# Router logits in two halves, the first expert block gathered by channel halves, and one table for three further blocks

## The reference

```python
hn = rms_norm(x, norm_ffn[1])                      # (256, 1024)
logits = hn @ w_router                             # (256, 8)
top_logit, top_idx = lax.top_k(logits, 2)
gate = softmax(top_logit)
# tokens of each expert are laid into blocks; for each block, with its expert e:
y_blk = (silu(x_blk @ w1[e]) * (x_blk @ w3[e])) @ w2[e]     # w1, w3: 1024x2816, w2: 2816x1024
y[token] += gate * y_blk
x = x + y
```

## Time and profile before

| | us |
|---|---|
| median of 3 runs | 1583.64 |
| lowest and highest | 1582.43, 1583.94 |
| the profiled execution, its time | 1583.63 |
| the profiled execution, its span | 1581.8 |
| TensorE busy | 1483.3 (94%) |
| VectorE busy | 1241.0 (78%) |
| ScalarE busy | 895.2 (57%) |
| last projection matmul starts | 739.15 |
| first expert matmul starts | 766.16 |

### The profile page before, as it was taken

How to read it: one execution, slowest core, us unless ns; L and a number is a source line. 1 busy time by engine, 2 the same in 40 slices (tenths; PEclk the granted TensorE clock), 3 DMA queues, 4 the chain that set the end, 5 groups by cost and what they waited for, 6 DMA issues and landing times.

```text
span 1581.8 us, 21845 instructions
## 1 busy us (share of the span) xinstructions
PE 1483.3 (94%) x7397; PEld 1201.7 (76%) x7397; DVE 1241.0 (78%) x1325; ACT 895.2 (57%) x970; POOL 388.1 (25%) x490
## 2 busy tenths in 40 slices
PE   4989989999998999999899999999999999999996
PEld 3767768788877776677688888888888888888785
DVE  6888967655555789856688988889888898888986
ACT  5632344544455523244476776767767677776774
POOL 6979972910002299900000000000000000000000
PEclk9989999999998999998899999999999999999998
DMA  9421235565544412077399999999999999999980
GB/s 263 161 80 54 80 82 185 182 198 178 191 160 141 134 54 80 28 252 254 129 364 345 348 361 333 351 344 339 362 331 351 345 339 361 331 351 327 355 293 27
DMA packets 269146, 373.48 MB, mean 236 GB/s; under 512 B 12960, under 2 KB 216096, under 8 KB 268960
## 3 DMA queue, kind: packets, MB, share of 16 engines
q1 hardware_dynamic: 265520, 366.47, 68.5%
q0 software_dynamic: 1280, 3.16, 1.0%
q10 hardware_dynamic: 2288, 3.11, 0.6%
HBM read 371.65 MB, written 1.05 MB: 236 GB/s over the span
## 4 chain that ended last, share of the span: by engine, by line
PE 72%; DVE 16%; ACT 5%; issue 4%; POOL 1%; DMA 0%; DVEq 0%; ACTq 0%; POOLq 0%
PE bank L459 69%; DVE lo L1204 4%; ACT hi L864 3%; DVE raw L1303 2%; PE bank L477 1%; DVE raw L1284 1%; PE bank L794 1%; DVE raw L1283 1%; DVE bank L1294 1%; DVE raw L1293 1%; POOL raw L330 1%; DVE at_lo L1640 1%; DVE bank L1295 1%; DVE bank L1296 1%; DVE at_lo L1609 1%
## 5 line engine op out<-in xcount | busy, mean ns | idle before, releaser
L1204 DVE TENSOR_TENSOR lo<-raw,hi 128x2048 fp32r<-128x2048 f32 x347 | 804.5, 2323 | 168.9 <-ACT hi L864 159.6
L864 ACT ACTIVATE hi<-raw 128x2048 fp32r<-128x2048 f32 x347 | 662.9, 1914 | 92.3 <-PE bank L459 91.8
L459 PE MATMUL bank<-hi,at_hi 128*128 128x512 f32 x1280 | 521.2, 407 | 31.8 <-DVE at_lo L1609 7.8
L459 PE MATMUL bank<-hi,at_lo 128*128 128x512 f32 x1280 | 506.4, 396 | 0.0
L459 PE MATMUL bank<-lo,at_hi 128*128 128x512 f32 x1280 | 506.3, 396 | 0.0
L459 PEld LDWEIGHTS bank<-hi,at_hi 128*128 128x128 f32 x1280 | 245.1, 191 | 85.4 <-issue 18.0
L459 PEld LDWEIGHTS bank<-hi,at_lo 128*128 128x128 f32 x1280 | 244.6, 191 | 52.9
L459 PEld LDWEIGHTS bank<-lo,at_hi 128*128 128x128 f32 x1280 | 245.4, 192 | 46.8
L459 PE MATMUL bank<-hi,ht_hi 128*128 128x512 f32 x440 | 172.2, 391 | 4.5 <-DVE ht_lo L1541 3.5
L459 PE MATMUL bank<-lo,ht_hi 128*128 128x512 f32 x440 | 171.3, 389 | 0.0
L459 PE MATMUL bank<-hi,ht_lo 128*128 128x512 f32 x440 | 171.2, 389 | 0.0
(11 more groups left out here) (235 smaller groups left out, 1177.7 us busy)
## 6 DMA issues: line engine op xcount, KB each, us to landing
raw<-in_moe_w_dram SPq DMA_DIRECT2D x528, 512.0 KB, 5.6
raw<-in_ffn_w_dram SPq DMA_DIRECT2D x66, 512.0 KB, 4.3
raw<-in_w_in_dram SPq DMA_DIRECT2D x64, 512.0 KB, 4.7
raw<-in_w_branch_dram SPq DMA_DIRECT2D x16, 512.0 KB, 4.0
raw<-in_w_out_dram SPq DMA_DIRECT2D x16, 512.0 KB, 4.5
raw<-in_w_glu_dram SPq DMA_DIRECT2D x4, 512.0 KB, 4.0
xres<-in_x_dram SPq DMA_DIRECT2D x1, 1024.0 KB, 5.3
areg<-in_norm_mix_dram ACTq DMA_DIRECT2D x2, 512.0 KB, 5.6
```

The lines of the kernel that those rows point to most:

```text
L459: return pe.matmul(o, a, b, start=start, stop=stop)
L864: act.activation(hi[:, slot, :], src, ACT.Copy).then_inc(hi_ready, 1)
L1204: tt(lo[:, slot, :], src, hi[:, slot, :].bitcast(f32), SUB).then_inc(lo_ready, 1)
```

## The change

1. The logits go into bank 2 (`PY[0]`) and the slot numbers into bank 3 (`PY[1]`), with semaphores of their own (`logits_full`, `pos_full`), in place of two turns of the TR banks. `logits(0)` issues the 16 matmuls on channel blocks 0 to 3 before `norm_t(1, "h", 1)`, and `logits(1)` those on blocks 4 to 7 after the last `at_lo`.
2. `gather` raises `xe_full` after each bank. ScalarE and VectorE wait for, and report, each half by itself. TensorE waits for half 0 before `up(0, 0, 0)` and for half 1 before `up(0, 0, 1)`. In the loop it waits for both halves at the place of before, with counts twice as high.
3. The table: in place of three rounds of eight small instructions, all three further blocks are handled in each instruction, over 24 or 48 numbers in place of 8 or 16.

```diff
--- before.py
+++ after.py
@@ -63,7 +63,6 @@
                 names.append((l, "o", s - 1))
         names += [(l, "a", t) for t in range(2)] + [(l, "s", t) for t in range(2)] + [(l, "s2", t) for t in range(2)]
         names += [(l, "m", g) for g in GROUPS] + [(l, "h", g) for g in GROUPS]
-    names += ["router", "pos"]
     return {name: n for n, name in enumerate(names)}
 
 
@@ -201,6 +200,7 @@
         h_full, g_ready, h_done, ht_tr, ht_hi_ready, ht_lo_ready = (sem("h_full"), sem("g_ready"), sem("h_done"), sem("ht_tr"),
                                                                     sem("ht_hi_ready"), sem("ht_lo_ready"))
         ffn_done = sem("ffn_done")
+        logits_full = sem("logits_full")
         sel_ready, pos_full, routed, final_ready, stored = (sem("sel_ready"), sem("pos_full"), sem("routed"),
                                                             sem("final_ready"), sem("stored"))
         gate_exp, router_in, place_ready, pg_full, gt_ready = (sem("gate_exp"), sem("router_in"), sem("place_ready"),
@@ -312,9 +312,11 @@
         r_hot = piece(384, 32).rearrange("p (i t e) -> p i t e", i=2, t=2)
         sel = piece(416, 16).rearrange("p (t e) -> p t e", t=2)
         r_pos = piece(432, 16).rearrange("p (t e) -> p t e", t=2)
-        r_over, r_rank, r_one = piece(448, 8), piece(456, 8), piece(464, 8)
+        r_over, r_rank = piece(448, 8), piece(456, 8)
         r_tmp = piece(472, 16).rearrange("p (t e) -> p t e", t=2)
         r_tab = piece(488, 5)
+        x_one, x_name = (piece(c, 24).rearrange("p (k e) -> p k e", k=3) for c in (576, 600))
+        x_tmp = piece(624, 48).rearrange("p (t k e) -> p t k e", t=2, k=3)
         router = piece(512, 64).rearrange("p (k e) -> p k e", k=KD)
         router_parts = ht_hi[:, 0, 0:KD * 2 * NE].rearrange("p (k c) -> p k c", k=KD)
         place = vreg[:, 1, 0:256].rearrange("p (t s) -> p t s", t=2)
@@ -741,25 +743,30 @@
             mixer(1)
 
 
+            def logits(half):
+
+                for th in range(TH):
+                    for k in range(4 * half, 4 * half + 4):
+                        for i, a in enumerate((at_hi, at_lo)):
+                            m = mm(PY[0][:, th * 16:(th + 1) * 16], a[:, k, th * P:(th + 1) * P], router_parts[:, k, :],
+                                   k + th + i == 0, th + i == 2 and k == KD - 1)
+                return m
+
+            pe.wait_ge(at_lo_ready, at_count(1, "h", 2))
+            pe.wait_ge(router_ready, 1)
+            logits(0)
             norm_t(1, "h", 1)
             pe.wait_ge(at_lo_ready, at_count(1, "h", 3))
-            pe.wait_ge(router_ready, 1)
-            bank = open_turn("router")
-            for th in range(TH):
-                for k in range(KD):
-                    for i, a in enumerate((at_hi, at_lo)):
-                        m = mm(bank[:, th * 16:(th + 1) * 16], a[:, k, th * P:(th + 1) * P], router_parts[:, k, :],
-                               k == 0 and i == 0, k == KD - 1 and i == 1)
-            m.then_inc(tr_full, 1)
+            logits(1).then_inc(logits_full, 1)
             pe.wait_ge(sel_ready, 1)
-            bank = open_turn("pos")
+            bank = PY[1]
             pe.wait_ge(loads, 32)
             tri, ones = cst[:, C_TRI:C_TRI + P], cst[:, C_ONE:C_ONE + P]
             mm(bank[:, 0:8], tri, sel[:, 0, :], True, True)
             mm(bank[:, 8:16], tri, sel[:, 1, :], True, False)
             mm(bank[:, 8:16], ones, sel[:, 0, :], False, True)
             mm(bank[:, 16:24], ones, sel[:, 0, :], True, False)
-            mm(bank[:, 16:24], ones, sel[:, 1, :], False, True).then_inc(tr_full, 1)
+            mm(bank[:, 16:24], ones, sel[:, 1, :], False, True).then_inc(pos_full, 1)
 
 
             def gather():
@@ -768,7 +775,8 @@
                     for th in range(TH):
                         m = mm(banks[4 + k // 4][:, (k % 4) * P:(k % 4 + 1) * P], xn[:, th, k * P:(k + 1) * P],
                                place[:, th, :], th == 0, th == 1)
-                m.then_inc(xe_full, 1)
+                    if k % 4 == 3:
+                        m.then_inc(xe_full, 1)
 
             def up(b, c, half):
 
@@ -778,7 +786,7 @@
                 if half == 0 and c == NCH - 1:
                     pe.wait_ge(gt_ready, b + 1)
                 if half == 0 and c == NCH:
-                    pe.wait_ge(xe_lo_ready, b + 2)
+                    pe.wait_ge(xe_lo_ready, 2 * b + 4)
 
                 for k in range(4):
                     m = three(h_bank(c)[:, :], at_hi[:, 4 * half + k, 0:P], at_lo[:, 4 * half + k, 0:P],
@@ -840,8 +848,8 @@
 
             pe.wait_ge(place_ready, 1)
             gather()
-            pe.wait_ge(xe_lo_ready, 1)
             for half in range(2):
+                pe.wait_ge(xe_lo_ready, half + 1)
                 up(0, 0, half)
             expert_step(0, 0)
             last = pe.value_load(table[0:1, 0:1], min_val=NE - 1, max_val=MAXB - 1)
@@ -1142,10 +1150,10 @@
             act.activation(r_exp, r_diff, ACT.Exp).then_inc(gate_exp, 1)
 
             def gathered(n):
-                act.wait_ge(xe_full, n)
                 for g in range(2):
-                    m = act.activation(at_hi[:, 4 * g:4 * g + 4, 0:P], banks[4 + g][:, :].rearrange("p (k c) -> p k c", k=4), ACT.Copy)
-                m.then_inc(xe_hi_ready, 1)
+                    act.wait_ge(xe_full, 2 * n + (g - 1))
+                    act.activation(at_hi[:, 4 * g:4 * g + 4, 0:P], banks[4 + g][:, :].rearrange("p (k c) -> p k c", k=4),
+                                   ACT.Copy).then_inc(xe_hi_ready, 1)
 
             def silu(b, c):
                 act.wait_ge(tile_used, b * FFN_TILES + (T_MOE + (3 * c if c > 0 else 1) + 1))
@@ -1566,11 +1574,11 @@
 
             for th in range(TH):
                 ts(xn[:, th, :], xn[:, th, :], col(RI + th), None, MUL).then_inc(xn_scaled, 1)
-            bank = wait_turn(dve, "router")
+            dve.wait_ge(logits_full, 1)
+            bank = PY[0]
             sums = bank[:, 0:32].rearrange("p (t i e) -> p t i e", t=2, i=2)
             own.step(dve.tensor_copy(r_tmp, sums[:, :, 0, :]))
-            tt(r_logit, r_tmp, sums[:, :, 1, :], ADD).then_inc(tr_free[TURN["router"] % 2], 1)
-            wait_read(dve, "router")
+            own.step(tt(r_logit, r_tmp, sums[:, :, 1, :], ADD))
             for th in range(TH):
                 own.step(dve.max(r_best[:, th, :], r_logit[:, th, :]))
                 own.step(dve.max_index(r_index[:, th, :], r_best[:, th, :], r_logit[:, th, :]))
@@ -1590,13 +1598,14 @@
             for i, g in enumerate((r_g, r_exp)):
                 own.step(tt(r_hot[:, i, :, :], r_hot[:, i, :, :], g.unsqueeze(2).broadcast_to([P, 2, NE]), MUL))
             own.step(tt(cols[:, 1, :, 0:NE], r_hot[:, 0, :, :], r_hot[:, 1, :, :], ADD))
-            bank = wait_turn(dve, "pos")
+            dve.wait_ge(pos_full, 1)
+            bank = PY[1]
             pos = bank[:, 0:16].rearrange("p (t e) -> p t e", t=2)
             own.step(stt(r_pos, pos, 1.0, sel, ADD, MUL))
             own.step(ts(cols[:, 0, :, 0:NE], r_pos, -1.0, None, ADD))
 
-            ts(r_over, bank[:, 16:24], float(P), None, ALU.is_gt).then_inc(tr_free[TURN["pos"] % 2], 1)
-            wait_read(dve, "pos")
+            own.step(ts(r_over, bank[:, 16:24], float(P), None, ALU.is_gt))
+
             def places():
 
                 for th in range(TH):
@@ -1604,28 +1613,27 @@
                 return m
 
             def gathered(n):
-                dve.wait_ge(xe_hi_ready, n)
                 for g in range(2):
-                    m = tt(at_lo[:, 4 * g:4 * g + 4, 0:P], banks[4 + g][:, :].rearrange("p (k c) -> p k c", k=4),
-                           at_hi[:, 4 * g:4 * g + 4, 0:P].bitcast(f32), SUB)
-                m.then_inc(xe_lo_ready, 1)
+                    dve.wait_ge(xe_hi_ready, 2 * n + (g - 1))
+                    tt(at_lo[:, 4 * g:4 * g + 4, 0:P], banks[4 + g][:, :].rearrange("p (k c) -> p k c", k=4),
+                       at_hi[:, 4 * g:4 * g + 4, 0:P].bitcast(f32), SUB).then_inc(xe_lo_ready, 1)
 
             own.step(dve.tensor_copy(column, cols[:, :, :, 0]))
             places().then_inc(place_ready, 1)
             own.step(dve.tensor_tensor_scan(r_rank, cst[:, C_ONE:C_ONE + NE], r_over, 0.0, MUL, ADD))
+            own.step(tt(x_one, r_rank.unsqueeze(1).broadcast_to([P, 3, NE]),
+                        cst[:, C_IOTA + 1:C_IOTA + 4].unsqueeze(2).broadcast_to([P, 3, NE]), ALU.is_equal))
+            ts(r_pos, cols[:, 0, :, 0:NE], 1000.0 - P, None, ADD)
+            own.step(tt(x_one, x_one, r_over.unsqueeze(1).broadcast_to([P, 3, NE]), MUL))
+            own.step(tt(x_name, x_one, experts_row.unsqueeze(1).broadcast_to([P, 3, NE]), MUL))
+            own.step(dve.tensor_reduce(r_tab[:, 2:5], x_name, AX.X, ADD))
+            for i, values in enumerate((r_pos, cols[:, 1, :, 0:NE])):
+                own.step(tt(x_tmp, values.unsqueeze(2).broadcast_to([P, 2, 3, NE]),
```

(16 more changed lines are left out.)

## The result

The changed kernel takes 1574.38 us (median of 6 runs, 1573.0 to 1575.91) against 1583.58 us (median of 6, 1582.43 to 1586.1): ratio 0.9942, 95% interval 0.9929 to 0.9954, so 9.2 us less. The forecast was 1575.8 us in a range of 1572.5 to 1579.0.

A forecast was written before the change was run, and what follows sets the result against it. The prediction took the kernel to be bound by TensorE, busy 94% of the span, and the edited passage by a serial chain of engine hops. Its terms, -3.4 - 2.5 - 1.9 = -7.8 us, gave 1575.8 us, range 1572.5 to 1579.0.

The forecast's parts named there:

- (a): Router logits in two halves, 16 of 32 matmuls moved ahead of the last transposes: -3.4 us, ends -4.5 and -1.3.
- (b): First expert block gathered by channel halves, so expert matmuls follow the gather at once: -2.5 us.
- (c): First 24 expert matmuls: TensorE's clock stays full without the idle time after the gather, -1.9 us.
- The cover: Behind the gather: first half subtracted 2.1 us before its end; 12 matmuls, 2.7 us, hide the second half's 1.4 us.
- (d): Table of the three further blocks at once, on VectorE beside the gather: 0, with 0 to -0.5 us as ends.
- (e): Two semaphore steps instead of one in every loop turn: 0, ends 0 to +1 us over seven turns.
- The clock is full for longer: Rival, 22%: full clock over the second router half and earlier in the gather; -10.2 us, 1573.4 us.
- The clock does not hold into the expert matmuls: Rival, 20%, also covering a late first half: only the router and gather halves gain, -5.9 us, 1577.7 us.
- The halves do not overlap: Rival, 5%: ScalarE or VectorE kept from the gather's first half until the gather is over; 1580.2 to 1581.5 us.
- the loop pays for each half: Rival, 3%: the second wait lengthens TensorE's wait in each loop turn; at 1.5 us per turn, 1586.3 us.

The follow-up runs named there:

- whole gather: Changed kernel, but with one semaphore step for all gather matmuls and for all of at_hi and at_lo, as before; ratio 0.9974 to the kernel before.
- whole router block: Changed kernel, but with all 32 router matmuls together behind the last at_lo; 1577.19 us, ratio 0.9965 to the kernel before.
- early copy and split: Changed kernel, but ScalarE copies the fourth tile before the first SiLU and VectorE splits it before the first hidden rows; 1574.74 us, ratio 0.9945 to before.

## Why the prediction was right

The bottleneck was read right: the change lies in a passage in which nothing runs beside anything longer, and all behind it moved up as it stood. By its steps:

(a) *-3.4, measured -3.85.* The first half cost nothing: it ran at full clock right behind the projection and the last at_lo was used 4.62 us into the passage, 4.66 before. The figure took all 16 remaining matmuls at 1.2 GHz; the first 0.5 us of them ran at 2.4 GHz, as the clock fell only at 745.7. Undone alone it gives back 3.45, where the 32 matmuls too ran in part at the full clock.

(b) and (c) *-2.5 and -1.9, measured -3.33 and -1.65.* The wait of 2.50 us went whole, and undone alone it brings back the low clock as well, 4.23 us together, where the two terms make 4.4. What was mis-sized in (b) is the gather, which I held at its old length: the clock rose 4.9 us into it, not 6.2, and it took 6.18 us, not 6.76, which is 0.6 more; the other 0.25 is that the first expert matmul, without a wait, starts before the gather's last matmul ends (760.36 and 760.61). The cover was thinner than I had it: the first subtraction ends 1.0 us before the gather does (759.57), not 2.1, since the clock rose in the gather's second half, and bank 4 was copied only 3.8 us into 6.2. In (c) I compared 7.37 us with a piece of 5.47 from the middle of a stream; at its start 24 matmuls take 5.75 to the SiLU.

(d) *0, measured -0.5.* The mechanism was as written, the first subtraction behind the old table, but I held it against a gather of 6.8 us; it took 6.1. The bound of -0.5 was the answer; 0 was wrong by that much. That the table is worth nothing by itself is shown by the whole gather with the old table (34.26 us).

(e) *0, measured -0.05 us a turn*, 0.35 in seven. No price for the second step. In the turn at 957 us TensorE starts 0.05 us after VectorE's subtraction ends, in the turn at 964 us of before 0.14 us. With the whole gather, with either table, the turn is 100.09 and the seven waits are 5.3 us in all, as before, against 4.6, so this gain comes with the halves. Why TensorE starts sooner I did not find out.

Sum: -8.86 - 0.35 = -9.2 us, which is what the medians differ by. That fit is closer than the data allow: the profiled executions differ by 7.7 us, and the changed kernel run again by 8.0 in the medians.

*The rivals.* "The clock is full for longer" was right in direction and had both its places, the second router half and the gather, but neither went the whole way: 1.0 us (0.45 and 0.6) of its 2.4. These 1.0 us are not shown to be the change's. With the whole router block TensorE has its old gaps, and the clock fell 5.5 us into the passage; with early copy and split the first of them is filled, and it fell at 3.4 us, as in the kernel before. At the lengths which the router half and the gather had in that kernel, the changed passage would be 7.8 us shorter than before, not 8.86. So the mechanism of the forecast is shown, by the kernels with one part undone, but that the total lies above it and not on it may be chance, and errors of both signs in (b) and (c) partly cancel. The Trainium skill's rule ("TensorE: Matmul & The Clock Gate", section "Why this matters for your kernels"), that without a long idle gap TensorE keeps its clock, does not hold in this passage: with the gaps filled, the clock fell in the middle of 2.5 us without any idle time. "The clock does not hold into the expert matmuls" did not occur: all of them took 0.39 to 0.40 us after the first. "The halves do not overlap" and "the loop pays for each half" were wrong.

## What to carry to other kernels

Where a chain hops between engines, the halves of a step pay when the last engine of the chain has work for the first half while the second travels; count what each engine does in between, since a side task that was free (the table) comes onto the path once the waits before it are gone. A wait of TensorE costs its own length and then whatever runs at the lower clock behind it, here 2.5 us and 1.5 to 1.6 us. When an ablation is worth less than the spread of the runs, measure the stretch itself in each trace from a common start.

## What was not expected of the hardware

The clock of TensorE fell although it was busy: during and right behind the 16 router matmuls (745.7 after the change, about 752.1 with the gaps filled). The fall and the rise come at different points of the program from one execution to the next: the second router half took 3.12 to 3.60 us in the kernels without added matmuls, the gather 6.08 to 6.76 us (the kernel before among them), with the same instructions. Filling gaps with matmuls that nobody reads is worth 3.6 us in the passage (30.11 to 26.51) and 1.7 to 4.5 us in the medians. It did not keep the clock up in any of the three kernels that have it in all gaps: where the fall came inside the added matmuls, it cost little, and where it came at the gather, 1.5 us (5.39 against 3.84).
